# Two transformer blocks on one core: feed-forward rows left undivided by their rms, relu on ScalarE and one square on VectorE, narrower scores of the first row tile

## The chip, the cores and the metric

The kernel runs on one core of a Trainium2 chip. The metric is the device time of one execution in microseconds (us), median over runs. All arithmetic is fp32 in accuracy: an operand is kept as the sum of a high and a low part (`..._hi`, `..._lo`) of the type fp32r, and one product becomes three TensorE matmuls, high by high, high by low and low by high.

## The reference

512 rows of width 1024 go through two blocks. What the change touches is the end of the second block and its windowed attention:

```python
# nsa_mixer: scores of query rows against keys, causal
s_s = jnp.einsum('bqghd,bgqkd->bghqk', qb, k_sel) * scale
s_w = jnp.einsum('bqghd,bkgd->bghqk', qb, kwb) * scale
...
# second_block
x = x + merged @ w_out[l]
h = rms_norm_2(x, norm_mlp[l])          # x * rsqrt(mean(x*x) + eps) * gain
x = x + jnp.square(jax.nn.relu(h @ w_ff1[l])) @ w_ff2[l]
return rms_norm_2(x, norm_final)
```

`w_ff1` is 1024 by 4096 and `w_ff2` 4096 by 1024. With r = rsqrt(mean(x*x) + eps) of a row, relu(r·a)² = r²·relu(a)².

## The kernel before

The hidden width of 4096 is worked off in 8 strips of 512 columns, t = 0 to 7. For a strip, TensorE (PE) multiplies the turned and gained rows by a strip of `w_ff1` in 96 matmuls of 128x512 (`ff_up`, L1111) into four banks of PSUM. VectorE (DVE) makes the activations `h_raw` (shown in the profile as `proj`) from the banks in two passes: `hidden` (L3327) writes max(bank, 0)·r², `square` (L3335) multiplies that by max(bank, 0) again. The factor r² stands in `r_squared`, 128x512, the rows' factors spread over the columns' order of the banks: DVE spreads them into `r_cols`, PE turns these (four transposes of L1034 in the middle of `ff_up(0)`), ScalarE (ACT) copies the bank (L2510) and DVE squares it (L3418).

The second multiplication, rows of `h_raw` by a 512-row strip of `w_ff2`, is done by a Strassen-like scheme of seven products of half-size blocks, twelve matmuls of 128x512 each, in the order 6, 1, 7, 5, 4, 2, 3 (`seven_products`, L1795). The rows' sums and the weights' sums that it needs are made on DVE (`row_sums`, `weight_sums`), their high parts on ACT (`rows_hi`: `a_hi`, `s_hi`; `items_hi`: `item_hi`), their low parts on DVE (`rows_lo`, `weights_lo`, five `item_lo`) and on GpSimd (POOL: the other two `item_lo`, L985). Each finished product lies in two banks, from which DVE adds it into the residual rows or into partial sums (`add_product`, L3355 and L3359). Partial sums are put together at the end (L3436, L3440); the last strip, t = 7, is an ordinary product.

All engines run the same software-pipelined loop, one step per t. PE does `ff_up(t+1)`, then `seven_products(t)`; each engine's order is the order in which its code is written, and semaphores tie them. What a step of DVE, ACT and PE says:

```python
# DVE, ff_step
add_product(i, lambda j: t(j) - 1, 3, 4 * parity)
row_sums(i, t); weight_sums(i, t); rows_lo(i, t); weights_lo(i, t)
hidden(i, lambda j: t(j) + 1)
add_product(i, t, 6, two)
square(i, lambda j: t(j) + 1)
add_product(i, t, 1, one); add_product(i, t, 7, two)
# PE, seven_products: product 5 writes the banks of strip t+1, product 4 those of 6 and 7
elif m == 5:
    pe.wait_ge(sem["emptied_d"], at(i, lambda j: strips_emptied("D", STRIP_FF + 1 + t(j))))
elif m == 4:
    taken(3)
```

`taken(3)` waits until DVE has added three products of this step: 6, 1 and 7. At the end of ACT's step, `his` makes the high parts of four pieces of `w_ff1` for strip t+2 (L1871); each piece comes by a transfer that SP starts when PE has used up the piece before it in the same buffer, four buffers in all. POOL then makes the low parts of the four pieces (L852).

In the attention of the second block, `LARGE_SMALL` units score a row tile i against its keys, as a high-by-high and a high-by-low set of matmuls (L1203, L1205), at least 256 keys wide.

Of the kernel before, what the change touches and what calls it, by code (L numbers as in the profile page):

```python
# [36 lines left out]
P = 128  # L37
# [57 lines left out]
STRIPS = ("A" * 12 + "D" + "AAAA" + "D" + "DD" + "DDDD" * 2 + "DD" + "A" * 6 + "D" * 8 + "DD"  # L95
          + "D" * 8 + "DD")

# [162 lines left out]
def two_block_kernel(  # L260
# [4 lines left out]
    with ExitStack() as ctx:  # L265
# [118 lines left out]
        for name, src, w in (("qb", g_qn_b[0:1, 64:96], 0), ("kb", g_kn_b[0:1, 64:96], 32),  # L384
# [4 lines left out]

        r_squared = place("r_squared", [P, S], where=A)  # L390
        kcv = place("kcv", [32, 2, 2, 64], where=A)
# [16 lines left out]
        stat2 = place("stat2", [P, 32])  # L408
        newton = place("newton", [P, 64])
        kr_sq = place("kr_sq", [P, TT])  # L410
        rstd = place("rstd", [P, 64])
# [33 lines left out]
            "group_done", "group_a", "group_d",  # L445
            "squares", "sq_made", "cq_squares", "b_squares", "mean_made", "root_made", "gate_half", "x_added", "x_turned", "xt_hi", "xt_lo", "r1_spread", "first_half_hi", "gate1_tanh", "r_spread", "r_turned", "r_kept", "gate_tanh", "tile_done", "stat_of", "pow_of", "stat_ready", "pow_done", "dve_step", "sin_in", "sin_out", "half_set",
            "ready_for_t", "qk_ready", "cq_ready", "b_ready", "kc_ready", "q_ready", "ix_scores", "ix_relu", "ix_acc", "z_scaled", "z_ready", "z_tanh",
# [3 lines left out]
            "tanh_in", "tanh_out", "flats", "hid_in", "h_hi", "h_lo", "h_summed", "half_sums",  # L451
            "quarter_in0", "quarter_in1", "quarter_in2", "quarter_in3", "t_made", "item_hi", "item_lo", "item_lo_p", "u_made", "r_squared", "product_done", "product_added", "sums_joined",
            "zeros_set", "keys_twice", "chunk_in0", "chunk_in1", "chunk_summed", "chunk_hi", "chunk_lo", "chunk_out0", "chunk_out1", "row_sums", "sums_hi", "sums_lo", "out_added",
# [551 lines left out]
        def _(pe):  # L1005
# [793 lines left out]
            def seven_products(i, parity, t):  # L1799
# [7 lines left out]
                for m in PRODUCTS:  # L1807
# [28 lines left out]
            def ff_step(i, parity, t):  # L1836

                if not isinstance(i, int):
# [4 lines left out]
                  before=raw_parts(2))  # L1843
            pe.wait_ge(sem["r_kept"], 1)

            ff_step(0, 0, lambda j: 0)
# [16 lines left out]
        def _(act):  # L1863
# [653 lines left out]
            def rows_hi(i, t):  # L2517

                act.wait_ge(sem["emptied_d"], at(i, lambda j: strips_emptied("D", STRIP_FF + t(j))))
                if not isinstance(i, int):  # L2520
# [28 lines left out]
            act.wait_ge(sem["emptied_d"], strips_emptied("D", STRIP_FF + 7))  # L2549
            act.wait_ge(sem["pair_used"], PAIR_LAST)  # L2550
# [28 lines left out]
        def _(dve):  # L2579
# [557 lines left out]
            def add_and_turn(n, s, v):  # L3137
# [16 lines left out]
                dve.wait_ge(sem["pow_done"], powers[0])  # L3154
                dve.tensor_copy(r_cols[:], rstd[:, 0:4].unsqueeze(2).to_broadcast([P, TT, P])).then_inc(sem["r_spread"], 1)

# [163 lines left out]

            def hidden(i, f):

                banks = strip_wait(i, lambda j: STRIP_FF + f(j))
                wait(dve, sem["h_hi"], at(i, lambda j: 3 * f(j)))
                wait(dve, sem["h_lo"], at(i, lambda j: 3 * f(j)))
                for m in range(4):
                    ins = dve.scalar_tensor_tensor(h_raw[:, m, :], banks[m][:], 0.0, r_squared[:], ALU.max, ALU.mult)  # L3327
                ins.then_inc(sem["u_made"], 1)

            def square(i, f):  # L3330

                banks = strip_wait(i, lambda j: STRIP_FF + f(j))
                dve.wait_ge(sem["u_made"], at(i, lambda j: f(j) + 1))
                for m in range(4):
# [12 lines left out]
            def add_product(i, t, m, banks):  # L3347

                dve.wait_ge(sem["product_done"], at(i, lambda j: 7 * t(j) + PRODUCTS.index(m) + 1))
                for u in range(2):  # L3350
# [26 lines left out]
            def row_sums(i, t):  # L3377

                dve.wait_ge(sem["emptied_d"], at(i, lambda j: strips_emptied("D", STRIP_FF + t(j))))
                dve.tensor_tensor(h_sums[:, 2], a11, a21, ALU.subtract)  # L3380
# [11 lines left out]
            def ff_step(i, parity, t):  # L3392
# [40 lines left out]
            dve.wait_ge(sem["product_added"], 49)  # L3433
            upper, lower = proj[:, 0:2, XRES:XRES + D], proj[:, 2:4, XRES:XRES + D]
# [4 lines left out]
            for v, z in ((upper[:, :, S:D], 1), (lower[:, :, S:D], 2)):  # L3439
                ins = dve.tensor_tensor(v, v, part_sums[z][:], ALU.add)  # L3440
            ins.then_inc(sem["sums_joined"], 1)
            dve.wait_ge(sem["sums_joined"], 2)
# [14 lines left out]
            for t in range(TT):  # L3457
                dve.wait_ge(sem["tile_done"], t + 1)
                for k in range(2):
                    v = proj[:, t, XRES + S + 256 * k:XRES + S + 256 * k + 256]  # L3460
                    dve.tensor_tensor(v, v, bank[4 * ((STRIP_LAST + 1) % 2) + t][:, 256 * k:256 * k + 256], ALU.add)\
                       .then_inc(sem["x_added"], 1)
# [39 lines left out]
```

## Time and profile before

| | us |
|---|---|
| median of 3 runs | 1413.48 (1412.42 to 1413.65) |
| the profiled execution | 1412.28 |
| its span in the trace | 1410.5 |
| PE busy | 1400.9 (99% of the span) |
| DVE, ACT, POOL busy | 895.0, 659.6, 634.7 |
| mean granted TensorE clock | 0.998 of full speed |

The span is the time from the first to the last recorded instruction; the execution's own time holds 1.8 us more. Times in the rows are microseconds from the start of the span. Feed-forward runs from about 1072 to 1404.

### The profile page before, as it was taken

To read this page: it belongs to the slowest core of one execution; us is meant where nothing else is said; L and a number is where in the kernel's file an instruction comes from. 1 tells how busy PE (TensorE), PEld (TensorE's weight loads), DVE (VectorE), ACT (ScalarE), POOL (GpSimd) and SP (SyncE) were. 2 spreads that over 40 slices of the span, in tenths; PEclk is the share of its full clock that TensorE was granted. 3 is DMA by queue.
4 is the path that set the end of the run, shared out by engine and by line. 5 is a ranking of instruction groups with operands and counts; after the bars stand their busy time and mean duration, and the time that the engine had idled before them with its cause. 6 is when DMAs were issued, how large, how long until landed. Compare 5 with 4: busy or idle time off the path is not lost.

```text
span 1410.5 us, 20863 instructions
## 1 busy us (share of the span) xinstructions
PE 1400.9 (99%) x7659; PEld 1182.9 (84%) x7659; DVE 895.0 (63%) x1646; ACT 659.6 (47%) x1157; POOL 634.7 (45%) x447
## 2 busy tenths in 40 slices
PE   9999999999999999999999999999999999999998
PEld 8888888778778888899997789988888888888886
DVE  4436998466663384852567678852283977777777
ACT  5544465567573333353343677863235443322342
POOL 4443666645453454154443366754425432344440
PEclk9999999999999999999999999999999999999999
DMA  6332433203102675869672210023275333333221
GB/s 196 99 90 75 148 105 101 66 13 104 37 2 75 209 240 196 292 199 318 237 243 75 76 31 2 2 76 105 90 271 188 114 99 105 104 104 104 91 87 60
DMA packets 90201, 170.28 MB, mean 121 GB/s; under 512 B 8119, under 2 KB 24066, under 8 KB 90114
## 3 DMA queue, kind: packets, MB, share of 16 engines
q1 hardware_dynamic: 80386, 140.72, 31.7%
q10 hardware_dynamic: 9728, 28.39, 5.5%
q8 instruction: 56, 0.92, 0.3%
q14 instruction: 31, 0.25, 0.1%
HBM read 148.12 MB, written 20.97 MB: 120 GB/s over the span
## 4 chain that ended last, share of the span: by engine, by line
PE 99%; DVE 0%; issue 0%; POOL 0%; ACT 0%; POOLq 0%; DVEq 0%; ACTq 0%
PE bank L1111 62%; PE bank L1795 9%; PE bank L1173 5%; PE bank L1387 5%; PE bank L1379 4%; PE bank L1203 4%; PE bank L1034 3%; PE bank L1205 1%; PE bank L1071 1%; PE bank L1612 0%; PE bank L1321 0%; PE bank L1783 0%; PE bank L1339 0%; PE bank L1424 0%; PE bank L1280 0%
## 5 line engine op out<-in xcount | busy, mean ns | idle before, releaser
L852 POOL TENSOR_TENSOR w_lo<-raw,w_hi 128x1024 fp32r<-128x1024 f32 (+3 forms) x185 | 442.7, 2402 | 455.0 <-ACT w_hi L1871 454.7
L1871 ACT ACTIVATE w_hi<-raw 128x1024 fp32r<-128x1024 f32 (+3 forms) x189 | 191.3, 1014 | 361.5 <-DMA raw<-in_w_in 166.0
L1111 PE MATMUL bank<-xt_hi,w_hi 128*128 128x512 f32 x656 | 258.8, 394 | 0.0
L1111 PE MATMUL bank<-xt_hi,w_lo 128*128 128x512 f32 x656 | 255.5, 390 | 0.0
L1111 PE MATMUL bank<-xt_lo,w_hi 128*128 128x512 f32 x656 | 255.4, 389 | 0.0
L1111 PE MATMUL bank<-w_hi,xt_hi 128*128 128x392 f32 (+2 forms) x424 | 153.6, 362 | 0.0
L1111 PE MATMUL bank<-w_lo,xt_hi 128*128 128x392 f32 (+2 forms) x424 | 151.8, 358 | 0.0
L1111 PE MATMUL bank<-w_hi,xt_lo 128*128 128x392 f32 (+2 forms) x424 | 151.8, 358 | 0.0
L1111 PEld LDWEIGHTS bank<-xt_hi,w_hi 128*128 128x128 f32 x656 | 123.2, 188 | 27.0 <-issue 2.4
L1111 PEld LDWEIGHTS bank<-xt_hi,w_lo 128*128 128x128 f32 x656 | 123.1, 188 | 25.8
L1111 PEld LDWEIGHTS bank<-xt_lo,w_hi 128*128 128x128 f32 x656 | 123.3, 188 | 25.2 <-issue 0.5
L985 POOL TENSOR_TENSOR item_lo<-quarter_b,item_hi 128x1024 fp32r<-128x1024 f32 x14 | 33.3, 2400 | 170.8 <-DVE item_lo L3389 170.8
L1111 PEld LDWEIGHTS bank<-w_hi,xt_hi 128*128 128x128 f32 x424 | 79.6, 188 | 7.2 <-issue 0.9
L1111 PEld LDWEIGHTS bank<-w_hi,xt_lo 128*128 128x128 f32 x424 | 79.6, 188 | 6.8
L1111 PEld LDWEIGHTS bank<-w_lo,xt_hi 128*128 128x128 f32 x424 | 79.6, 188 | 6.1
L2137 ACT ACTIVATE sc<-sc,negmax 128x512 f32<-128x512 f32 (+3 forms) x104 | 58.8, 567 | 21.5 <-DVE negmax L2846 21.3
L3355 DVE TENSOR_TENSOR proj<-proj,bank 128x512 f32<-128x512 f32 x56 | 36.0, 683 | 38.7 <-PE bank L1795 38.7
L896 POOL TENSOR_SCALAR proj<-proj,rsum,gsig 128x384 f32<-128x384 f32 (+1 forms) x64 | 38.7, 614 | 40.1 <-DVE rsum L2861 40.1
L2846 DVE CUSTOM_DVE_ANT_0 sc<-bank,cst 128x128 f32<-128x128 f32 (+3 forms) x96 | 43.6, 485 | 15.9 <-PE bank L1203 9.7
L2137 ACT ACTIVATE proj<-proj,negmax 128x384 f32<-128x384 f32 (+1 forms) x80 | 44.0, 552 | 10.5 <-DVE negmax L2846 10.4
L2522 ACT ACTIVATE a_hi<-proj 128x1024 fp32r<-128x1024 f32 x7 | 7.4, 1063 | 85.0 <-PE bank L1795 85.0
L1034 PE MATMUL bank<-cst,proj 128*128 128x128 f32 (+2 forms) x320 | 44.7, 280 | 0.3
(460 smaller groups left out, 3006.7 us busy)
## 6 DMA issues: line engine op xcount, KB each, us to landing
raw<-in_w_in SPq DMA_DIRECT2D x72, 512.0 KB, 3.6
raw<-in_w_ff SPq DMA_DIRECT2D x36, 512.0 KB, 3.7
quarter_b<-in_w_ff SPq DMA_DIRECT2D x28, 512.0 KB, 3.4
raw<-in_w_in SPq DMA_DIRECT2D x24, 392.0 KB, 4.6
w_hi<-sums_hi SPq DMA_DIRECT2D x16, 512.0 KB, 5.0
w_lo<-sums_lo SPq DMA_DIRECT2D x16, 512.0 KB, 5.9
raw<-in_w_branch SPq DMA_DIRECT2D x12, 512.0 KB, 3.7
chunk_a<-in_w_out ACTq DMA_DIRECT2D x12, 512.0 KB, 5.4
```

Of the source, the lines that this page charges most:

```text
L852: pool.tensor_tensor(w_lo[:, slot, 0:halves, 0:width], raw[:, slot, 0:halves, 0:width], w_hi[:, slot, 0:halves, 0:width].bitcast(F32), ALU ...
L896: pool.tensor_scalar(v, v, rsum[:, u % SC:u % SC + 1], gate, ALU.mult, ALU.mult)\
L1034: ins = pe.transpose(b[0:m, o:o + k], src, ident[0:k, 0:k])
L1111: ins = pe.matmul(o, lhs, rhs, start=st and j == 0, stop=en and j == 2)
L1173: ins = pe.matmul(bank[OUT_BANK[m] + u][:], rows[:, 2 * q + kk, u * P:u * P + P], whole[:, slot, kk, :], start=m in (1, 7, 4, 6) and q == ...
L1203: ins = pe.matmul(o, w["q"], w["k"], start=True, stop=w["k_lo"] is None)
L1379: ins = pe.transpose(bank[TURN_BANK + u % 2][0:n, c + t * P:c + (t + 1) * P], src[:, t * P:t * P + n], ident)
L1387: ins = pe.matmul(bank[4 + w["pas"] % 2][w["rows"], w["cols"]], w["v"][t], src[0:n, t * P:(t + 1) * P], start=w["start"] and t == 0, stop= ...
L1795: ins = pe.matmul(bank[banks + u][:], lhs, rhs, start=first and kt == 0 and j == 0, stop=kt == 1 and j == 2, skip_group_check=True)
L1871: act.activation(w_hi[:, slot, 0:halves, 0:width], raw[:, slot, 0:halves, 0:width], ACT.Copy)\
L2137: act.activation(v, v, ACT.Exp, scale=-1.0, bias=negmax[:, u % SC:u % SC + 1], accum_out=sums[:, u % SC:u % SC + 1]).then_inc(sem["exps"], 1)
L2846: dve.tensor_tensor_reduce(sc_of[u % SC][:, 0:w["n"]], bank[b][:, c:c + w["n"]], w["mask"], -w["scale"], BIG, ALU.add, ALU.min, negmax[:, ...
```

## The change

The hidden rows are no longer multiplied by r². ACT writes h = relu(bank) in four instructions 128x512 at the start of its step, before `rows_hi`, then raises the semaphore `relu`; DVE squares `h_raw` in one instruction over 128x4x512 that reads and writes SBUF alone. The factor r² of each row, now 4 columns of the tile `newton`, is put on where the products are added to the residual rows: `add_product` for 2, 3, 4 and 5, the joining of partial sums, and the last strips' additions become a multiply-add with a scalar per row. The spreading of r over rows, its four transposes, its copy and its square (L3418) go. The banks of a feed-forward strip are now given back by ACT, and PE's product 5 waits for that. ACT's loop over t takes two steps an iteration. Scores of the first row tile are 128 keys wide in place of 256, in 32 units of a high and a low matmul each.

```diff
-          + "D" * 8 + "DD")
+          + "A" * 8 + "DD")
...
-            k_hi, k_lo = (part[:, 0:max(i + 1, 2) * P] for part in keys2[g][kind - 1])
+            k_hi, k_lo = (part[:, 0:(i + 1) * P] for part in keys2[g][kind - 1])
...
-                    if r == 2 and kt == 7:
-                        pe.wait_ge(sem["r_spread"], 2)
-                        transposes([(r_cols[:, t, :], P, P) for t in range(TT)])(bank[4]).then_inc(sem["r_turned"], 1)
...
-                        pe.wait_ge(sem["emptied_d"], at(i, lambda j: strips_emptied("D", STRIP_FF + 1 + t(j))))
+                        pe.wait_ge(sem["emptied_a"], at(i, lambda j: strips_emptied("A", STRIP_FF + 1 + t(j))))
...
-            act.wait_ge(sem["r_turned"], 1)
-            act.activation(r_rows[:], bank[4][:], ACT.Copy).then_inc(sem["r_kept"], 1)
...
+            def hidden(i, f):
+
+                banks = strip_wait(i, lambda j: STRIP_FF + f(j))
+                wait(act, sem["h_lo"], at(i, lambda j: 3 * f(j)))
+                wait(act, sem["h_summed"], at(i, f))
+                for m in range(4):
+                    ins = act.activation(h_raw[:, m, :], banks[m][:], ACT.Relu)
+                    if m == 3:
+                        ins.then_inc(sem["emptied_a"], 1)
+                act.wait_ge(sem["emptied_a"], at(i, lambda j: strips_emptied("A", STRIP_FF + f(j))))
+                act.sem_inc(sem["relu"], 1)
...
                 if isinstance(i, int):
                     items_hi(i, t)
+                hidden(i, t)
                 rows_hi(i, t)
...
-            with act.Fori(1, 7) as i:
-                ff_step(i, lambda j: j)
+            with act.Fori(1, 4) as i:
+                ff_step(i, lambda j: 2 * j - 1)
+                ff_step(i, lambda j: 2 * j)
+            hidden(7, lambda j: j)
...
-                    dve.tensor_tensor(v, v, banks[t][:], ALU.add).then_inc(sem["x_added"], 1)
+                    dve.scalar_tensor_tensor(v, banks[t][:], r_squared[:, t:t + 1], v, ALU.mult, ALU.add)\
+                       .then_inc(sem["x_added"], 1)
...
             def square(i, f):
 
-                banks = strip_wait(i, lambda j: STRIP_FF + f(j))
-                dve.wait_ge(sem["u_made"], at(i, lambda j: f(j) + 1))
-                for m in range(4):
-                    ins = dve.scalar_tensor_tensor(h_raw[:, m, :], banks[m][:], 0.0, h_raw[:, m, :], ALU.max, ALU.mult)
-                ins.then_inc(sem["emptied_d"], 1)
+                dve.wait_ge(sem["relu"], at(i, lambda j: f(j) + 1))
+                dve.tensor_tensor(h_raw, h_raw, h_raw, ALU.mult).then_inc(sem["h_made"], 1)
...
                     if o is not None:
-                        ins = dve.tensor_tensor(o, o, bank[banks + u][:], ALU.add)
+                        r = 2 * (m in (4, 5)) + u
+                        ins = dve.scalar_tensor_tensor(o, bank[banks + u][:], r_squared[:, r:r + 1], o, ALU.mult, ALU.add)
...
                 weights_lo(i, t)
-                hidden(i, lambda j: t(j) + 1)
                 add_product(i, t, 6, two)
                 square(i, lambda j: t(j) + 1)
...
-            dve.wait_ge(sem["r_kept"], 1)
-            dve.tensor_tensor(r_squared[:], r_rows[:], r_rows[:], ALU.mult).then_inc(sem["r_squared"], 1)
-            dve.wait_ge(sem["r_squared"], 1)
-            hidden(0, lambda j: 0)
             square(0, lambda j: 0)
...
-            for v, z in ((upper[:, :, S:D], 0), (lower[:, :, 0:S], 0), (lower[:, :, S:D], 0)):
-                ins = dve.tensor_tensor(v, v, part_sums[z][:], ALU.add)
-            ins.then_inc(sem["sums_joined"], 1)
+            def join(z, row, c):
+
+                for u in range(2):
+                    t = 2 * row + u
+                    v = proj[:, t, XRES + S * c:XRES + S * c + S]
+                    ins = dve.scalar_tensor_tensor(v, part_sums[z][:, u, :], r_squared[:, t:t + 1], v, ALU.mult, ALU.add)
+                return ins
```

On ACT, at the seam between two steps of the feed-forward loop, before: the four `w_hi` end step 0 and the next step begins with the rows' high parts (`a_hi`, `s_hi`), then the weights' (`item_hi`).

```order
L2525 ACTIVATE s_hi<-h_sums 128x2048
L1871 ACTIVATE w_hi<-raw 128x1024 x4
L2547 UNCONDITIONAL_BRANCH
L2547 ISA
L2521 REGISTER_ALU
L2522 ACTIVATE a_hi<-proj 128x1024
L2523 ACTIVATE a_hi<-proj 128x512
L2524 REGISTER_ALU
L2525 ACTIVATE s_hi<-h_sums 128x2048
```

And in the changed kernel, at the seam of the two steps inside an iteration (`proj` written from `bank` is `h_raw`):

```order
L1865 ISA
L1866 ACTIVATE w_hi<-raw 128x1024 x2
L1885 REGISTER_ALU
L2526 ACTIVATE proj<-bank 128x512 x4
L2529 REGISTER_ALU
L2512 REGISTER_ALU
L2515 ACTIVATE a_hi<-proj 128x1024
L2516 ACTIVATE a_hi<-proj 128x512
L2518 ACTIVATE s_hi<-h_sums 128x2048
```

The four relus of strip t+1 stand behind the last `w_hi` of step t and ahead of that strip's `a_hi`.

On DVE, in the middle of a step of the loop, from the last `item_lo` to the additions, before (`proj` is `h_raw` in L3327 and L3335, the residual rows in L3355; `part_sum_124`, `_123`, `_125` take products 6, 1, 7):

```order
L3389 TENSOR_TENSOR item_lo_108<-quarter_t_101,item_hi_109 128x1024
L2593 REGISTER_ALU
L3327 SCALAR_TENSOR_TENSOR proj<-bank,r_squared 128x512 x4
L3359 TENSOR_TENSOR part_sum_124<-part_sum_124,bank 128x512 x2
L3333 REGISTER_ALU
L3335 SCALAR_TENSOR_TENSOR proj<-bank,proj 128x512 x4
L3359 TENSOR_TENSOR part_sum_123<-part_sum_123,bank 128x512 x2
L3359 TENSOR_TENSOR part_sum_125<-part_sum_125,bank 128x512 x2
L3355 TENSOR_TENSOR proj<-proj,bank 128x512 x4
```

And in the changed kernel:

```order
L3390 TENSOR_TENSOR item_lo_108<-quarter_t_101,item_hi_109 128x1024
L3360 TENSOR_TENSOR part_sum_124<-part_sum_124,bank 128x512 x2
L3335 REGISTER_ALU
L3336 TENSOR_TENSOR proj<-proj 128x4x512
L3360 TENSOR_TENSOR part_sum_123<-part_sum_123,bank 128x512 x2
L3360 TENSOR_TENSOR part_sum_125<-part_sum_125,bank 128x512 x2
L3356 SCALAR_TENSOR_TENSOR proj<-bank,newton,proj 128x512 x4
```

The eight passes over the banks are gone; one square stands between the addition of product 6 and those of 1 and 7, which stay behind it.

On PE, the scores of the first row tile of a pair of heads in the second block, before:

```order
L1203 MATMUL bank<-k_parts,q_parts 128x512
L1205 MATMUL bank<-k_parts,q_parts 128x512
L1203 MATMUL bank<-k_parts,q_parts 128x256
L1205 MATMUL bank<-k_parts,q_parts 128x256
L1203 MATMUL bank<-k_parts,q_parts 128x256
L1205 MATMUL bank<-k_parts,q_parts 128x256
L1111 MATMUL bank<-beside,w_hi 128x512 x2
```

And in the changed kernel:

```order
L1200 MATMUL bank<-k_parts,q_parts 128x512
L1202 MATMUL bank<-k_parts,q_parts 128x512
L1200 MATMUL bank<-k_parts,q_parts 128x128
L1202 MATMUL bank<-k_parts,q_parts 128x128
L1200 MATMUL bank<-k_parts,q_parts 128x128
L1202 MATMUL bank<-k_parts,q_parts 128x128
L1111 MATMUL bank<-beside,w_hi 128x512 x2
```

The count and the order stay; four matmuls in a row are half as wide.

## Rows read from the trace of the kernel before

**Rows 1.** The page: busy time, share of the span and instructions of each engine.

```profile
PE 1400.9 (99%) x7659; PEld 1182.9 (84%) x7659; DVE 895.0 (63%) x1646; ACT 659.6 (47%) x1157; POOL 634.7 (45%) x447
```

**Rows 2.** The chain that ended last, step t = 2: start, us, what.

```profile
1199.68 19.04 PE bank L1795 x84
```

**Rows 3.** Timeline of DVE in that step: start, us, operation; in brackets idle before, releaser.

```profile
1199.72 2.48 DVE L3327 SCALAR_TENSOR_TENSOR proj<-bank,r_squared 128x512 f32<-128x512 f32 x4 [3.41 <-PE bank L1111]
1202.44 1.28 DVE L3359 TENSOR_TENSOR part_sum<-part_sum,bank 128x512 f32<-128x512 f32 x2 [0.24 <-PE bank L1795]
1203.64 2.48 DVE L3335 SCALAR_TENSOR_TENSOR proj<-bank,proj 128x512 f32<-128x512 f32 x4
...
1207.88 1.28 DVE L3359 TENSOR_TENSOR part_sum<-part_sum,bank 128x512 f32<-128x512 f32 x2 [0.57 <-PE bank L1795]
```

**Rows 4.** Timeline of ACT there: the last `w_hi` of the step.

```profile
1203.41 1.06 ACT L1871 ACTIVATE w_hi<-raw 128x1024 fp32r<-128x1024 f32 x1 [4.24 <-DMA raw<-in_w_ff]
```

**Rows 5.** Timeline of ACT, an eviction of four banks by ACT in the first block.

```profile
150.82 2.07 ACT L1912 ACTIVATE proj<-bank 128x512 f32<-128x512 f32 x4 [0.26 <-PE bank L1111]
```

**Rows 6.** Groups of DVE by line and form: count | busy, mean ns of one.

```profile
L3345 DVE TENSOR_TENSOR s_lo<-h_sums,s_hi 128x2048 fp32r<-128x2048 f32 x7 | 16.0, 2283 | 0.5 <-ACT s_hi L2525 0.5
L3335 DVE SCALAR_TENSOR_TENSOR proj<-bank,proj 128x512 f32<-128x512 f32 x32 | 19.8, 680 | 0.1
```

**Rows 7.** Timeline of POOL in step t = 2.

```profile
1201.19 9.49 POOL L852 TENSOR_TENSOR w_lo<-raw,w_hi 128x1024 fp32r<-128x1024 f32 x4
```

**Rows 8.** Timelines of DVE and POOL elsewhere, operations of SBUF alone on both.

```profile
1097.36 2.89 DVE L3418 TENSOR_TENSOR r_squared<-r_rows 128x512 f32<-128x512 f32 x1
...
1096.72 2.97 POOL L852 TENSOR_TENSOR w_lo<-raw,w_hi 128x1024 fp32r<-128x1024 f32 x1 [4.51 <-ACT w_hi L1871]
...
512.64 2.90 DVE L3165 TENSOR_TENSOR chunk_a<-chunk_a 128x512 f32<-128x512 f32 x1
...
512.34 5.45 POOL L852 TENSOR_TENSOR w_lo<-raw,w_hi 128x1024 fp32r<-128x1024 f32 x2 [3.03 <-ACT w_hi L1871]
```

**Rows 9.** The chain that ended last around strip 0 and the first products.

```profile
1093.12 0.44 PE bank L1034 x4
...
1118.08 19.04 PE bank L1795 x84
```

**Rows 10.** Timelines of ACT and DVE in step t = 0.

```profile
1105.85 2.00 ACT L2536 ACTIVATE item_hi<-quarter_b 128x1024 fp32r<-128x1024 f32 x2
...
1109.21 1.90 ACT L2525 ACTIVATE s_hi<-h_sums 128x2048 fp32r<-128x2048 f32 x1
...
1105.38 0.69 DVE L3380 TENSOR_TENSOR h_sums<-proj 128x512 f32<-128x512 f32 x1
1107.43 0.69 DVE L3383 TENSOR_TENSOR h_sums<-proj,h_sums 128x512 f32<-128x512 f32 x1
1113.36 1.22 DVE L3389 TENSOR_TENSOR item_lo<-quarter_t,item_hi 128x1024 fp32r<-128x1024 f32 x1
```

**Rows 11.** Timeline of PE, scores of a first row tile.

```profile
827.52 0.28 PE L1203 MATMUL bank<-k_parts,q_parts 128*128 128x256 f32 x1
...
828.00 0.60 PE L1379 MATMUL bank<-cst,proj 128*128 128x128 f32 x4
```

**Rows 12.** Timeline of PE's weight loads (PEld): full weights for 16-column matmuls.

```profile
737.20 0.75 PEld L1673 LDWEIGHTS bank<-proj 128*128 128x128 f32 x6
```

**Rows 13.** Timeline of PE: 128-wide plain fp32 matmuls, four in the program, eight records.

```profile
413.30 1.05 PE L1387 MATMUL bank<-prob_t,kvm 128*128 128x128 f32 x8
```

**Rows 14.** Timeline of DVE at the end: the joining of sums and the next addition.

```profile
1384.63 3.50 DVE L3436 TENSOR_TENSOR proj<-proj,part_sum 128x1024 f32<-128x1024 f32 x3
...
1393.08 2.48 DVE L3090 TENSOR_TENSOR proj<-proj,bank 128x512 f32<-128x512 f32 x4 [2.56 <-PE bank L1111]
```

**Rows 15.** Windows after the last matmul: busy PE, PEld, DVE, ACT, POOL; PEclk (granted clock).

```profile
1404.00:1406.00 2.00, 0.00 (x0) 0.00 (x0) 1.93 (x6) 1.52 (x5) 0.13 (x1) 1.00 0.68 262
1406.00:1410.50 4.50, 0.00 (x0) 0.00 (x0) 0.57 (x2) 0.72 (x1) 0.54 (x1) 0.51 0.62 233
```

More of the change, by code:

```diff
@@ L388, in two_block_kernel @@
         allow = place("allow", [P, 1280 - P])
-        r_squared = place("r_squared", [P, S], where=A)
         kcv = place("kcv", [32, 2, 2, 64], where=A)
@@ L409, in two_block_kernel @@
         newton = place("newton", [P, 64])
+        r_squared = newton[:, 0:TT]
         kr_sq = place("kr_sq", [P, TT])
@@ L445, in two_block_kernel @@
             "group_done", "group_a", "group_d",
-            "squares", "sq_made", "cq_squares", "b_squares", "mean_made", "root_made", "gate_half", "x_added", "x_turned", "xt_hi", "xt_lo", "r1_spread", "first_half_hi", "gate1_tanh", "r_spread", "r_turned", "r_kept", "gate_tanh", "tile_done", "stat_of", "pow_of", "stat_ready", "pow_done", "dve_step", "sin_in", "sin_out", "half_set",
+            "squares", "sq_made", "cq_squares", "b_squares", "mean_made", "root_made", "gate_half", "x_added", "x_turned", "xt_hi", "xt_lo", "r1_spread", "first_half_hi", "gate1_tanh", "r_spread", "gate_tanh", "tile_done", "stat_of", "pow_of", "stat_ready", "pow_done", "dve_step", "sin_in", "sin_out", "half_set",
             "ready_for_t", "qk_ready", "cq_ready", "b_ready", "kc_ready", "q_ready", "ix_scores", "ix_relu", "ix_acc", "z_scaled", "z_ready", "z_tanh",
@@ L451, in two_block_kernel @@
             "tanh_in", "tanh_out", "flats", "hid_in", "h_hi", "h_lo", "h_summed", "half_sums",
-            "quarter_in0", "quarter_in1", "quarter_in2", "quarter_in3", "t_made", "item_hi", "item_lo", "item_lo_p", "u_made", "r_squared", "product_done", "product_added", "sums_joined",
+            "quarter_in0", "quarter_in1", "quarter_in2", "quarter_in3", "t_made", "item_hi", "item_lo", "item_lo_p", "relu", "h_made", "product_done", "product_added", "sums_joined",
             "zeros_set", "keys_twice", "chunk_in0", "chunk_in1", "chunk_summed", "chunk_hi", "chunk_lo", "chunk_out0", "chunk_out1", "row_sums", "sums_hi", "sums_lo", "out_added",
@@ L1843, in _ @@
                   before=raw_parts(2))
-            pe.wait_ge(sem["r_kept"], 1)
             ff_step(0, 0, lambda j: 0)
@@ L2517, in rows_hi @@
             def rows_hi(i, t):
-                act.wait_ge(sem["emptied_d"], at(i, lambda j: strips_emptied("D", STRIP_FF + t(j))))
+                act.wait_ge(sem["h_made"], at(i, lambda j: t(j) + 1))
                 if not isinstance(i, int):
@@ L2546, in _ @@
             ff_step(0, lambda j: 0)
-            with act.Fori(1, 7) as i:
-                ff_step(i, lambda j: j)
-            act.wait_ge(sem["emptied_d"], strips_emptied("D", STRIP_FF + 7))
+            with act.Fori(1, 4) as i:
+                ff_step(i, lambda j: 2 * j - 1)
+                ff_step(i, lambda j: 2 * j)
+            hidden(7, lambda j: j)
+            act.wait_ge(sem["h_made"], 8)
             act.wait_ge(sem["pair_used"], PAIR_LAST)
@@ L3154, in add_and_turn @@
                 dve.wait_ge(sem["pow_done"], powers[0])
-                dve.tensor_copy(r_cols[:], rstd[:, 0:4].unsqueeze(2).to_broadcast([P, TT, P])).then_inc(sem["r_spread"], 1)
+                if n == 0:
+                    dve.tensor_copy(r_cols[:], rstd[:, 0:4].unsqueeze(2).to_broadcast([P, TT, P])).then_inc(sem["r_spread"], 1)
+                else:
+                    step(dve.tensor_tensor(r_squared, rstd[:, 0:4], rstd[:, 0:4], ALU.mult))
             def sum_chunk(c):
@@ L3319, in _ @@
             a11, a12, a21, a22 = h_raw[:, 0:2, 0:256], h_raw[:, 2:4, 0:256], h_raw[:, 0:2, 256:512], h_raw[:, 2:4, 256:512]
-            def hidden(i, f):
-                banks = strip_wait(i, lambda j: STRIP_FF + f(j))
-                wait(dve, sem["h_hi"], at(i, lambda j: 3 * f(j)))
-                wait(dve, sem["h_lo"], at(i, lambda j: 3 * f(j)))
-                for m in range(4):
-                    ins = dve.scalar_tensor_tensor(h_raw[:, m, :], banks[m][:], 0.0, r_squared[:], ALU.max, ALU.mult)
-                ins.then_inc(sem["u_made"], 1)
-            def square(i, f):
-                banks = strip_wait(i, lambda j: STRIP_FF + f(j))
-                dve.wait_ge(sem["u_made"], at(i, lambda j: f(j) + 1))
-                for m in range(4):
-                    ins = dve.scalar_tensor_tensor(h_raw[:, m, :], banks[m][:], 0.0, h_raw[:, m, :], ALU.max, ALU.mult)
-                ins.then_inc(sem["emptied_d"], 1)
+            def square(i, f):
+                dve.wait_ge(sem["relu"], at(i, lambda j: f(j) + 1))
+                dve.tensor_tensor(h_raw, h_raw, h_raw, ALU.mult).then_inc(sem["h_made"], 1)
             def rows_lo(i, t):
@@ L3377, in row_sums @@
             def row_sums(i, t):
-                dve.wait_ge(sem["emptied_d"], at(i, lambda j: strips_emptied("D", STRIP_FF + t(j))))
+                dve.wait_ge(sem["h_made"], at(i, lambda j: t(j) + 1))
                 dve.tensor_tensor(h_sums[:, 2], a11, a21, ALU.subtract)
@@ L3433, in _ @@
             dve.wait_ge(sem["product_added"], 49)
-            upper, lower = proj[:, 0:2, XRES:XRES + D], proj[:, 2:4, XRES:XRES + D]
-            for v, z in ((upper[:, :, S:D], 0), (lower[:, :, 0:S], 0), (lower[:, :, S:D], 0)):
-                ins = dve.tensor_tensor(v, v, part_sums[z][:], ALU.add)
-            ins.then_inc(sem["sums_joined"], 1)
+            def join(z, row, c):
[4 more added lines that the diff above has]
+                return ins
+            join(0, 0, 1)
+            join(0, 1, 0)
+            join(0, 1, 1).then_inc(sem["sums_joined"], 1)
             dve.wait_ge(sem["sums_joined"], 1)
-            for v, z in ((upper[:, :, S:D], 1), (lower[:, :, S:D], 2)):
-                ins = dve.tensor_tensor(v, v, part_sums[z][:], ALU.add)
-            ins.then_inc(sem["sums_joined"], 1)
+            join(1, 0, 1)
+            join(2, 1, 1).then_inc(sem["sums_joined"], 1)
             dve.wait_ge(sem["sums_joined"], 2)
@@ L3460, in _ @@
                     v = proj[:, t, XRES + S + 256 * k:XRES + S + 256 * k + 256]
-                    dve.tensor_tensor(v, v, bank[4 * ((STRIP_LAST + 1) % 2) + t][:, 256 * k:256 * k + 256], ALU.add)\
+                    dve.scalar_tensor_tensor(v, bank[4 * ((STRIP_LAST + 1) % 2) + t][:, 256 * k:256 * k + 256],
+                                             r_squared[:, t:t + 1], v, ALU.mult, ALU.add)\
                        .then_inc(sem["x_added"], 1)
```

## The prediction

> **What bounds the kernel now.** I read the page first: TensorE is busy for 1400.9 of 1410.5 us [rows 1]. The chain that ended last says the same, and in the feed-forward loop it holds nothing but TensorE: a step's seven products (84 matmuls, 19.04 us, 0.2267 each) follow the matmuls of the strip without a piece of another engine between [rows 2]. So nothing that the change saves on VectorE, ScalarE or GpSimd shortens the kernel by itself. It can only win by matmuls removed or narrowed, and lose wherever TensorE has to wait. Of such waits the loop has two that the change touches. Product 5 waits until the banks of strip t+1 are empty, product 4 until three additions (6, 1, 7) are done. Counted from the start of the products, 1199.68, product 5 comes after 36 matmuls, at 1207.84, and product 4 after 48, at 1210.56 [rows 2]. The timeline of VectorE shows the third addition ending at 1207.88 + 1.28 = 1209.16, because it can't begin before product 7 is done [rows 3]. So 1.4 us are spare at product 4. That is all the room that the middle of the step has.
>
> **The middle of a step.** Before, VectorE worked through 2.48 + 1.28 + 2.48 us of passes and additions there, all from banks that TensorE had filled already [rows 3]. Now the square waits for the relus, and these stand in ScalarE's queue behind the last `w_hi` of the step. That one waits for its transfer, and runs from 1203.41 to 1204.47 [rows 4], long after strip t+1 was finished at 1199.68. The ring of four buffers behind it isn't changed, so it stays there. Four relus from banks: the nearest row is ScalarE's eviction of four banks of the same shape, 2.07 us [rows 5]. They run from 1204.4 to 1206.45; with about 0.1 us for the wait on their own end, the square may begin at 1206.6. Product 5, due at 1207.84, gets its banks 1.3 us in time.
>
> The square is one instruction with 2048 columns, both inputs and the output in SBUF. The nearest row, a subtraction of that shape, takes 2.28 us [rows 6]. Alone it would end at 1208.9. The additions of 1 and 7 stand behind it in VectorE's order, each some 1.2 us: the third ends at 1211.4. Product 4 would be 0.9 to 1.0 us late.
>
> But it isn't alone. GpSimd is making the low parts of four weight pieces from 1201.19 to 1210.68, 2.37 us each, so its third runs from 1205.93 to 1208.30 [rows 7]. What two such operations do to each other stands elsewhere in the trace. A 128x512 multiplication of VectorE, in SBUF alone, was begun at 1097.36 and took 2.89 us [rows 8], where one of that shape takes 0.69 [rows 10]; it ended half a microsecond after GpSimd's operation (1096.72 to 1099.69), as if it had only then begun. At 512.64 the same: 2.90 us beside two operations of GpSimd, which for their part took 2.73 each in place of 2.4 [rows 8]. The passes of before read a bank, and they ran beside those same low parts at 680 ns, with no such delay [rows 6, 7]. So I take it that the square, ready at 1206.6, begins when GpSimd's third operation ends, at 1208.3, and GpSimd's fourth begins when the square ends. Square until 1210.6, additions until 1213.0, product 4 at 1213.1 in place of 1210.5: TensorE stands for **2.6 us**. GpSimd's fourth low part ends at 1213 in place of 1210.7, and is wanted only in a later step, hidden. The Trainium skill, page "SBUF — State Buffer", section "Who interferes with whom", states the same as a rule: the port pair that VectorE's second SBUF input and GpSimd share is locked for a whole instruction. By it the stall is that of the locked square; without it, that of the free one. This trace agrees, with its 2.89 us.
>
> Steps 1 to 6 have this: 6 x 2.6 = **+15.6 us**. Every stall shifts all engines alike (transfers start from TensorE's progress), so none is paid for by the one before.
>
> **Step 0.** Four transposes go, 0.44 us [rows 9]. But `h_raw` of strip 0 is now made behind ScalarE's seven `item_hi`, which end at 1107.85 [rows 10], about 1107.4 once everything is 0.44 earlier. Relus until 1109.5 [rows 5], square until 1111.9 [rows 6]. Then the old row of steps: row sums 2.74 (1105.38 to 1108.12 before), `s_hi` 1.90 [rows 10], `s_lo` 2.28 [rows 6], the first `item_lo` 1.22: 1120.1 with a little for semaphores. TensorE is there at 1118.08 - 0.44 = 1117.64 [rows 9]. Before, that `item_lo` ended at 1114.6 [rows 10], so the 3.4 us of room are used up, and 2.5 more. The middle of step 0 has the same square with the rest of the step late; I take 0.6 us for it, between 0 and the 2.6 of other steps. Sum of step 0: 2.5 + 0.6 - 0.44 = **+2.7**.
>
> **Scores.** 32 units with a high and a low matmul, 64 in all, go from 256 to 128 columns. Four of 256 take 0.48 us, 0.12 each [rows 11]. How fast the narrow ones go isn't in the trace for this type. From below: if the time fell by width alone, from 0.227 at 512 and 0.12 at 256, it would be about 0.06, and 64 would save 3.8 us. From above: a plain fp32 product of 128 columns shows as two records, and eight of them, 1.05 us with the last one's length of 0.275, come every 0.11: 0.22 a product [rows 13]; if the narrow ones were run that way, they would cost 64 x 0.10 = 6.4 us more. Between them I take what a full set of weights costs when the moving side is tiny: six loads for matmuls of 16 columns in 0.75 us, with one's own length of 0.19, one every 0.11 [rows 12]. The narrow matmuls stand four in a row, each with weights of its own, so 64 x 0.007 = **-0.4 us**. The Trainium skill, page "TensorE: Matmul & The Clock Gate", section "LDWEIGHTS (loading the stationary operand)", has 107 ns for a load of 128 columns, which agrees with the 0.11. Its section "Back-to-back issue gap" has 81 ns a matmul at 128 columns in a sustained stream; by that the 64 would save 2.5 us in place of 0.4.
>
> **What lies beside other work, at nothing.** The factor in `add_product` makes a two-operand addition a three-operand one of the same shape with a bank: such a form took 2.48 us for four where the addition takes 1.28 for two [rows 3]. They are product 5, 4, 2, 3, after each of which VectorE waits for TensorE; without that cover it would be some 0.05 us each. The joins become ten of 0.6 where five took 1.17: 6.0 for 5.85 us, before 2.56 us of idle [rows 14]. The copy on ScalarE and L3418 go from engines that don't bound. The two-step loop on ScalarE changes nothing that it issues.
>
> **The clock.** After the last matmul (before 1404) the granted clock stayed at full up to 1406 and was half after that [rows 15]. Within the kernel no wait before was long enough to see it fall. Six waits of 2.6 us are at the edge of what that end shows. A fall puts matmuls at 1.2 GHz for a while, each taking twice as long, and how long is in no row: from nothing to another stall's length each, 0 to 15.6 in all. I take **+3**, a fifth of that.
>
> **Sum.** 1412.28 + 15.6 + 2.7 - 0.4 + 3 = 1433.2. The profiled execution lies 1.2 us under the median of 1413.48, so the median comes to 1434.
>
> **Rivals.**
> - A, forecast: the square waits behind GpSimd's third low part. For it, [rows 3 to 8]. Without the clock 1431.4, with all of its price 1447. Chance 0.62.
> - B: the square isn't held, because it gets in between two of GpSimd's operations or because the two don't exclude each other in this form. Stalls of 1.0 us: 6.0 + 2.7 - 0.4 = +8.3, 1421.8. For it, that the relus end within 0.7 us of GpSimd's second boundary, 1205.93; against it, that they would have to be 0.7 us earlier. Chance 0.15.
> - C: the narrow scores run like plain fp32, +6.4 on A in place of -0.4: 1438 to 1441. For it only that the code held them at 256. Chance 0.12.
> - D: no stall, because the relus are done early enough, say for a last transfer that lands 2.5 us sooner. The third addition then ends by 1210.5, and all that is left is under 3 us at step 0, or nothing: within 0.2%. Against it, [rows 4]. Chance 0.06.
> - E, the other side: the narrow scores gain by width, 3.8 us, and the loop doesn't stall. 1413.5 - 3.8 - 0.44 = 1409.3, if step 0 is hidden too. It decides if all stalls together stay under 1.4 us, which asks the third addition to end by 1210.5 in every step. Chance 0.05.
>
> **The numbers.** 0.2% of this kernel, 2.8 us, is about what a measurement can tell. A, B and C are slower, 0.89; D is same, 0.06; E is faster, 0.05. The range takes in B at its low end, 1421, and C and most of the clock's price at the upper end, 1443; D, E and a full fall of the clock are left out.
>
> **What would show it.** In the changed kernel's timeline each step has ScalarE's last `w_hi`, four relus about 2.07 us, a square of some 4.0 us in the records (begun at 1206.6 relative to a product start at 1199.68, its wait counted in), two additions, and a gap of 2.6 us on TensorE before product 4 that VectorE's L3360 released. If the square shows 2.3 us and the gap 1 us, it is B. If the matmuls of L1200 and L1202 of 128 columns come every 0.11 us, the scores are right; at 0.06 it is E's gain, at 0.2 C. At the first products a gap of 2.5 us, released by VectorE. I am wrong if ScalarE's last `w_hi` moves forward or back with the change, if relu costs other than a copy, or if the clock falls in most steps.

## The result and the profile after

The changed kernel takes 1436.78 us (median of 6 runs, 1435.66 to 1437.53), the kernel before 1412.89 (6 runs). The ratio is 1.017, with a 95% interval of 1.0159 to 1.0181: 24 us slower.

The page of the changed kernel, engines by busy time:

```profile
span 1434.8 us, 20823 instructions
PE 1405.2 (98%) x7655; PEld 1182.0 (82%) x7655; DVE 874.6 (61%) x1594; ACT 675.0 (47%) x1188; POOL 643.7 (45%) x447
```

VectorE works 20 us less than in [rows 1] and ScalarE 15 us more. Neither says anything of the 24 us. The chain that ended last does: where [rows 2] had nothing but TensorE, a step (t = 2) now reads

```profile
1206.74 3.75 DMA raw<-in_w_ff
1211.48 2.05 ACT proj L2526 x4
1213.60 3.87 DVE proj L3336
1217.47 2.40 DVE part_sum L3360 x4
1220.01 8.41 PE bank L1792 x36
```

The last weight piece lands, ScalarE makes its high part, then the relus; VectorE squares, adds products 1 and 7, and only then TensorE goes on, with product 4. ScalarE there, to be set beside [rows 4]:

```profile
1210.52 1.06 ACT L1866 ACTIVATE w_hi<-raw 128x1024 fp32r<-128x1024 f32 x1 [4.42 <-DMA raw<-in_w_ff]
1211.48 2.04 ACT L2526 ACTIVATE proj<-bank 128x512 f32<-128x512 f32 x4
```

The timelines of VectorE and GpSimd answer to [rows 3] and [rows 7]:

```profile
1209.33 1.28 DVE L3360 TENSOR_TENSOR part_sum<-part_sum,bank 128x512 f32<-128x512 f32 x2 [6.01 <-PE bank L1792]
1213.60 3.87 DVE L3336 TENSOR_TENSOR proj<-proj 128x2048 f32<-128x2048 f32 x1 [2.99 <-ACTq L2530]
1217.39 2.47 DVE L3360 TENSOR_TENSOR part_sum<-part_sum,bank 128x512 f32<-128x512 f32 x4
...
1208.19 11.50 POOL L852 TENSOR_TENSOR w_lo<-raw,w_hi 128x1024 fp32r<-128x1024 f32 x4
```

GpSimd's four operations take 11.50 us in place of 9.49. At 2.37 each the third ends at 1215.3, and 2.2 us after that, at 1217.47, the square ends, close to the 2.28 that it takes alone. The two don't share the time. The third operation of GpSimd, beside which the square's record begins, has 2.4 us in its own record, as when alone, and the fourth, beside the square, has 4.4. On TensorE's timeline the two matmuls on either side of the gap:

```profile
1217.07 0.39 PE L1792 MATMUL bank<-item_hi,s_lo 128*128 128x512 f32 x1
1220.01 0.47 PE L1792 MATMUL bank<-item_hi,a_hi 128*128 128x512 f32 x1 [2.56 <-DVE part_sum L3360]
```

Between their starts lie 2.94 us in place of the pitch of 0.23: 2.7 us lost. The same gap, 2.92 to 2.94, stands in each of steps 1 to 6, and one of 2.76 (from 1117.51 to 1120.27) before the first products. The clock fell after three of the seven. Windows behind the gap of step 5 (busy PE, PEld, DVE, ACT, POOL; PEclk):

```profile
1352.00:1353.00 1.00, 0.60 (x2) 0.53 (x3) 1.00 (x3) 0.00 (x0) 0.07 (x1) 0.74 0.00 0
1353.00:1355.00 2.00, 2.00 (x6) 1.53 (x5) 0.57 (x1) 0.00 (x0) 0.00 (x0) 0.50 0.00 0
1355.00:1356.00 1.00, 1.00 (x4) 0.79 (x3) 0.00 (x0) 0.00 (x0) 0.00 (x0) 0.55 0.00 0
1356.00:1358.00 2.00, 2.00 (x11) 1.60 (x10) 0.97 (x2) 0.00 (x0) 0.00 (x0) 1.00 0.00 0
```

Half clock, 1.2 GHz, for a little over 3 us. In the chain such a piece is longer for the same count of matmuls: 10.05 us for 36 (10.01 in step 3), where the four steps without a fall have 8.4, and 20.93 for the 84 of step 0. Before, these 84 took 19.2 us, counted in the same way from the start of the first of them (1117.92 on TensorE's timeline): 1.7 less.

```profile
1120.27 20.93 PE bank L1792 x84
...
1352.40 10.05 PE bank L1792 x36
```

### The profile page after: what moved, and what is told of

Same layout as the page of the kernel before. It is cut to its first block, busy times and chain, and to the rows that moved or that the text cites. A ratio compares the mean times of both kernels' runs of the same rounds, so it can differ in the third digit from the quotient of the medians.

```text
span 1434.8 us, 20823 instructions
## 1 busy us (share of the span) xinstructions
PE 1405.2 (98%) x7655; PEld 1182.0 (82%) x7655; DVE 874.6 (61%) x1594; ACT 675.0 (47%) x1188; POOL 643.7 (45%) x447
## 4 chain that ended last, share of the span: by engine, by line
PE 90%; DVE 4%; DMA 3%; ACT 2%; issue 1%; POOL 0%; SPq 0%; ACTq 0%; POOLq 0%; DVEq 0%
PE bank L1111 59%; PE bank L1173 5%; PE bank L1792 5%; PE bank L1384 4%; PE bank L1376 4%; PE bank L1200 4%; PE bank L1034 3%; DVE proj L3336 2%; DMA raw<-in_w_ff 2%; PE bank L1202 1%; PE bank L1071 1%; DVE part_sum L3360 1%; ACT proj L2526 1%; DMA raw<-in_w_in 1%; PE bank L1609 0%
## 5 line engine op out<-in xcount | busy, mean ns | idle before, releaser
L852 POOL TENSOR_TENSOR w_lo<-raw,w_hi 128x1024 fp32r<-128x1024 f32 (+3 forms) x185 | 449.3, 2437 | 459.8 <-ACT w_hi L1866 459.6
L2132 ACT ACTIVATE sc<-sc,negmax 128x512 f32<-128x512 f32 (+3 forms) x104 | 58.8, 566 | 20.9 <-DVE negmax L2854 20.5
L3356 DVE SCALAR_TENSOR_TENSOR proj<-bank,newton,proj 128x512 f32<-128x512 f32 x56 | 39.4, 744 | 34.1 <-PE bank L1792 34.1
L1792 PE MATMUL bank<-item_hi,a_hi 128*128 128x512 f32 x84 | 34.5, 411 | 15.2 <-DVE part_sum L3360 15.2
```

Of the source, the lines that this page charges most:

```text
L852: pool.tensor_tensor(w_lo[:, slot, 0:halves, 0:width], raw[:, slot, 0:halves, 0:width], w_hi[:, slot, 0:halves, 0:width].bitcast(F32), ALU ...
L1792: ins = pe.matmul(bank[banks + u][:], lhs, rhs, start=first and kt == 0 and j == 0, stop=kt == 1 and j == 2, skip_group_check=True)
L2132: act.activation(v, v, ACT.Exp, scale=-1.0, bias=negmax[:, u % SC:u % SC + 1], accum_out=sums[:, u % SC:u % SC + 1]).then_inc(sem["exps"], 1)
L3356: ins = dve.scalar_tensor_tensor(o, bank[banks + u][:], r_squared[:, r:r + 1], o, ALU.mult, ALU.add)
```

## The experiments

Seven kernels, each measured beside the kernel before on the same chip. Ratios are to that kernel.

### pool_yields: GpSimd keeps off until the square is done

```diff
                 for q in range(4):
+                    if q == 2 and made is not None:
+                        pool.wait_ge(sem["h_made"], at(i, made))
                     split(at(i, lambda j: p0(j) + q), (PAIR_FF + q) % RING, 2, S, PAIR_FF)
...
-                ff1_lo(i, lambda j: PAIR_FF + 8 + 4 * j)
+                ff1_lo(i, lambda j: PAIR_FF + 8 + 4 * j, lambda j: j + 2)
```

> The changed kernel, but in the loop GpSimd makes the third and fourth weight low of a step only after the square. Theory (the square is held by GpSimd's third operation): the square takes 2.3 us in place of 3.9, each of the six gaps of 2.9 us between matmul starts falls to 1.3, which is 1.6 x 6 = 9.6 us, and no gap of the loop is long enough for the clock to fall, 3.2 us more: about 1424 us. Rival (the square is slow in its own right, one operand read twice): it still takes 3.9 us and the time stays at 1437.

Measured: 1422.89 us, ratio 1.0075 (1.0058 to 1.0092). Timelines of VectorE and GpSimd in step 2:

```profile
1209.74 2.29 DVE L3338 TENSOR_TENSOR proj<-proj 128x2048 f32<-128x2048 f32 x1 [2.81 <-ACTq L2532]
1211.95 2.47 DVE L3362 TENSOR_TENSOR part_sum<-part_sum,bank 128x512 f32<-128x512 f32 x4
...
1206.85 2.41 POOL L852 TENSOR_TENSOR w_lo<-raw,w_hi 128x1024 fp32r<-128x1024 f32 x1
1212.20 4.74 POOL L852 TENSOR_TENSOR w_lo<-raw,w_hi 128x1024 fp32r<-128x1024 f32 x2 [2.93 <-DVE proj L3338]
```

With GpSimd idle the same square takes 2.29 us. The gaps of the loop are 1.18 to 1.33 us, one 0.86. The rival, a square that is slow by itself, is out: it was GpSimd's operation that held it for 1.6 us. What stays, about 1 us a step, is the relus' lateness and the order on VectorE. In the profiled execution, 1420.98 us, the clock never fell before the last matmul. The other three took 1422.87 to 1423.91; a fall would make such a difference, but no trace of them shows whether there was one.

### square_after_one: one addition less behind the square

```diff
                 add_product(i, t, 6, two)
-                square(i, lambda j: t(j) + 1)
                 add_product(i, t, 1, one)
+                square(i, lambda j: t(j) + 1)
                 add_product(i, t, 7, two)
```

> The changed kernel with the addition of product 1 ahead of the square. Theory (the two additions behind the square are part of each stall): the square ends where it did, one addition of 1.2 us less stands behind it, the gaps fall from 2.9 to 1.7 us: 7.2 us, and the two falls of the clock in the loop go, 3.2 us: about 1426. Rival (product 4 waits for something else than the third addition): 1437.

Measured: 1426.61 us, ratio 1.0097 (1.008 to 1.0114). VectorE, then the matmuls beside the gap:

```profile
1214.70 3.99 DVE L3336 TENSOR_TENSOR proj<-proj 128x2048 f32<-128x2048 f32 x1
1218.61 1.27 DVE L3360 TENSOR_TENSOR part_sum<-part_sum,bank 128x512 f32<-128x512 f32 x2
...
1218.30 0.39 PE L1792 MATMUL bank<-item_hi,s_lo 128*128 128x512 f32 x1
1220.03 0.47 PE L1792 MATMUL bank<-item_hi,a_hi 128*128 128x512 f32 x1 [1.34 <-DVE part_sum L3360]
```

The square is held as long as ever, the gap is 1.73 us in place of 2.94: the one addition that no longer stands behind it. The profiled execution, 1428.75, is the slowest of the four; it holds one more wait, 1.71 us between two starts at 1074.66, ahead of the feed-forward strips and of the edit.

### square_last: square behind all three additions

```diff
                 add_product(i, t, 6, two)
-                square(i, lambda j: t(j) + 1)
                 add_product(i, t, 1, one)
                 add_product(i, t, 7, two)
+                square(i, lambda j: t(j) + 1)
```

> The changed kernel with the square behind the additions of 6, 1 and 7. Theory: none of the six gaps is left, 16.2 us and the two falls of the clock 3.2 us: about 1417, with the gap of 2.8 us at the first products and its fall of the clock still there. Rival (a late square gives a new wait: the addition of product 5 or the row sums of the next step come late): a gap at product 3 or at the next products, 1 us or more a step, 1423 or more.

Measured: 1415.79 us, ratio 1.0023 (1.0014 to 1.0033). VectorE in step 2:

```profile
1211.36 1.28 DVE L3360 TENSOR_TENSOR part_sum<-part_sum,bank 128x512 f32<-128x512 f32 x2 [1.43 <-PE bank L1792]
1212.56 3.86 DVE L3336 TENSOR_TENSOR proj<-proj 128x2048 f32<-128x2048 f32 x1
1216.34 2.71 DVE L3356 SCALAR_TENSOR_TENSOR proj<-bank,newton,proj 128x512 f32<-128x512 f32 x4
1219.52 1.41 DVE L3356 SCALAR_TENSOR_TENSOR proj<-bank,newton,proj 128x512 f32<-128x512 f32 x2 [0.46 <-PE bank L1792]
```

The square is still held to 3.86 us, and TensorE doesn't notice: no gap of the loop is left. The additions behind it come late, but VectorE is idle again from 1219.05 to 1219.52, and no new wait appears. Only the gap before the first products is there, 2.75 us, and the low clock behind it.

### square_last_relu0: the relus of strip 0 ahead of the item highs

```diff
                 if isinstance(i, int):
+                    hidden(i, t)
                     items_hi(i, t)
-                hidden(i, t)
+                else:
+                    hidden(i, t)
                 rows_hi(i, t)
```

Beside this it has the order of square_last on VectorE.

> The kernel of square_last, with the relus of strip 0 on ScalarE ahead of the seven item highs of step 0. Theory (the gap before the first products is the relus' place behind the item highs): no gap of over 1 us is left from 1000 us on, 2.5 us of stall and about 2 us of low clock less than square_last: 1411.3, by 0.5 to 1.5 under the kernel before. Rival (step 0 is held by the chain from square over row sums and their parts, wherever the relus stand, or the item highs now come late): a gap of 1 us or more remains, 1413 or more.

Measured: 1411.81 us, ratio 0.9991 (0.9982 to 1.0). ScalarE in step 0, and TensorE at the seam of strip 1 and the first products:

```profile
1101.04 2.04 ACT L2526 ACTIVATE proj<-bank 128x512 f32<-128x512 f32 x4
1111.33 1.91 ACT L2518 ACTIVATE s_hi<-h_sums 128x2048 fp32r<-128x2048 f32 x1
...
1117.70 0.39 PE L1111 MATMUL bank<-xt_hi,w_lo 128*128 128x512 f32 x1
1117.92 0.39 PE L1792 MATMUL bank<-item_hi,s_hi 128*128 128x512 f32 x1
```

The relus run at 1101.0 in place of 1107.6, the first product follows its strip at the pitch, and no gap is left. The items are 2 us later than before and `s_hi` with them, within the room of step 0.

### relu_early: VectorE as changed, relus ahead of the last weight high

```diff
                 if isinstance(i, int):
+                    hidden(0, lambda j: 0)
                     items_hi(i, t)
-                hidden(i, t)
                 rows_hi(i, t)
...
-                his(i, lambda j: PAIR_FF + 8 + 4 * t(j))
+                his(i, lambda j: PAIR_FF + 8 + 4 * t(j), 3)
+                hidden(i, lambda j: t(j) + 1)
+                his(i, lambda j: PAIR_FF + 8 + 4 * t(j), 4, q0=3)
...
-            hidden(7, lambda j: j)
```

Here `his` got a first piece, `q0`, and the relus of strip 0 stand ahead of the item highs. So this run holds two moves; that the one in step 0 has its own effect, square_last and square_last_relu0 show.

> The changed kernel with VectorE's order as it was changed (square ahead of the additions of 1 and 7), but with the four relus between the third and the last weight high on ScalarE, and those of strip 0 ahead of the item highs. Theory (the relus' lateness behind the last weight high starts the stall): the square is ready 2.9 us sooner, is held by GpSimd's second operation in place of its third, and the third addition ends some 11 us after the start of the products, where product 4 is due: gaps of at most 0.5 us more than the pitch, no fall of the clock, 1411 to 1414. Rival (the held square alone makes the stall, wherever it begins): gaps of 1.5 us or more in each step, 1421 or more.

Measured: 1412.23 us, ratio 0.9996 (0.9987 to 1.0005). ScalarE, VectorE and GpSimd in step 2:

```profile
1199.53 2.07 ACT L2526 ACTIVATE proj<-bank 128x512 f32<-128x512 f32 x4 [0.80 <-PE bank L1111]
...
1203.32 2.28 DVE L3337 TENSOR_TENSOR proj<-proj 128x2048 f32<-128x2048 f32 x1
1207.55 1.28 DVE L3361 TENSOR_TENSOR part_sum<-part_sum,bank 128x512 f32<-128x512 f32 x2 [0.76 <-PE bank L1792]
...
1200.98 11.59 POOL L852 TENSOR_TENSOR w_lo<-raw,w_hi 128x1024 fp32r<-128x1024 f32 x4
```

The time came as expected, by a way that I had wrong. The square wasn't held by GpSimd's second operation: it came at 1203.32, just before that one began (1200.98 + 2.37 = 1203.35), took 2.28 us, and GpSimd did the waiting (11.59 for four in place of 9.49); so it went in all six steps, each time by 0.02 to 0.03 us. What it stood behind was no longer the relus, done at 1201.60, but the addition of product 6. The third addition waits for its product again, as in [rows 3], and TensorE has no gap in the loop or before it.

### factor_only: the factor at the outputs, both passes on VectorE

```diff
+                for m in range(4):
+                    ins = dve.tensor_scalar(h_raw[:, m, :], banks[m][:], 0.0, None, ALU.max)
+                ins.then_inc(sem["h_made"], 1)
...
-                dve.tensor_tensor(h_raw, h_raw, h_raw, ALU.mult).then_inc(sem["h_made"], 1)
...
+                for m in range(4):
+                    ins = dve.scalar_tensor_tensor(h_raw[:, m, :], banks[m][:], 0.0, h_raw[:, m, :], ALU.max, ALU.mult)
+                ins.then_inc(sem["emptied_d"], 1)
```

> The changed kernel with relu and square on VectorE from the banks in two passes, as before, but with the factor at the outputs and the narrow scores. Theory (the factor at the outputs is hidden beside other work): no gap anywhere, 1412 us, 0.5 to 1.5 under the kernel before. Rival (multiply-adds at the outputs cost 0.13 us a pair more and delay the end or a product): some 2 us or more over the kernel before.

Measured: 1411.85 us, ratio 0.9996 (0.9986 to 1.0006). TensorE has no gap in the feed-forward. A multiply-add with a scalar per row is dearer than an addition, at the end too. The last joins of the kernel before, which belong to [rows 14], then this kernel:

```profile
1388.16 2.36 DVE L3440 TENSOR_TENSOR proj<-proj,part_sum 128x1024 f32<-128x1024 f32 x2
```

```profile
1384.20 6.84 DVE L3436 SCALAR_TENSOR_TENSOR proj<-part_sum,newton,proj 128x512 f32<-128x512 f32 x10
1392.52 2.73 DVE L3084 SCALAR_TENSOR_TENSOR proj<-bank,newton,proj 128x512 f32<-128x512 f32 x4 [1.49 <-PE bank L1111]
```

Ten joins take 6.84 us where the five of before took 3.50 + 2.36; one microsecond of the idle time in [rows 14] is gone, 1.49 is left. So the factor, the transposes and the narrow scores together change nothing that can be measured.

### scores_alone: the narrow scores in the kernel before

```diff
-            k_hi, k_lo = (part[:, 0:max(i + 1, 2) * P] for part in keys2[g][kind - 1])
+            k_hi, k_lo = (part[:, 0:(i + 1) * P] for part in keys2[g][kind - 1])
```

> The kernel before with the narrower scores of the first row tile alone. My theory (weights set the pace): 0.11 us a matmul, 0.4 to 1.3 us less in all, inside what the measurement can tell. Rival by width: 3.8 us less, 1409. Rival (they are run in several passes): 6 us more, 1419.

Measured: 1411.86 us, ratio 0.9993 (0.9984 to 1.0002). TensorE at one group of four:

```profile
886.38 0.22 PE L1203 MATMUL bank<-projr 128*128 128x128 f32 x1
886.43 0.28 PE L1205 MATMUL bank<-projr 128*128 128x128 f32 x1
886.54 0.28 PE L1203 MATMUL bank<-projr 128*128 128x128 f32 x1
886.66 0.28 PE L1205 MATMUL bank<-projr 128*128 128x128 f32 x1
```

The second starts 0.05 us after the first, then one every 0.11 to 0.12. Both rivals, 1409 and 1419, are out, and so is the saving of 2.5 us that the prediction names beside its own sum.

The time can't tell so small a gain from zero, but the traces can. The same two matmuls of 512 columns, one ahead of these scores and one behind them, start at 819.98 and 937.96 before and at 819.41 and 937.04 here: 117.98 and 117.63 us apart. In the changed kernel it is 117.64, in square_last_relu0 117.63. The scores save 0.35 us, where 0.4 was forecast.

## Why the prediction was right, step by step

It was right in its mechanism, its sign and nearly its size: 1434 forecast, 1436.8 measured. The account in the trace, by spans (1410.5 to 1434.8, 24.3 us):

| term | forecast | seen |
|---|---|---|
| six stalls before product 4 | 6 x 2.6 = 15.6 | 6 x 2.8 = 16.8 |
| step 0: before the first products | 2.5 | 2.76 - 0.23 = 2.5 |
| step 0: its middle | 0.6 | none |
| step 0: transposes gone | -0.44 | -0.5 |
| low clock | 3 | 1.7 + 1.6 + 1.6 = 4.9 |
| scores | -0.4 | -0.35 |
| waits ahead of the feed-forward | none | 0.6 |
| sum | 20.9 | 24.0 |

The stalls are counted from strip to strip. In the chain, before and then changed:

```profile
1199.68 19.04 PE bank L1795 x84
1218.72 21.76 PE bank L1111 x96
...
1184.82 21.77 PE bank L1111 x96
...
1228.41 21.77 PE bank L1111 x96
```

A step takes 43.59 us in place of 40.80, 2.8 more; 2.7 of it is the gap between two starts, and 0.1 more goes with it. The transposes are read from two matmuls of `ff_up(0)` on either side of them, 1090.00 and 1100.02 before, 1090.31 and 1099.83 changed. The 0.6 us ahead of the feed-forward belong to no term of the change: the largest part is one wait of 0.5 us near 814, ahead of the scores, and it differs from run to run, from nothing in relu_early to 1.1 us in square_after_one. The 0.3 us that is left over stands in no term.

**The held square** was shown: with GpSimd quiet it takes 2.29 us, beside it 3.87. What the section "Who interferes with whom" of the page "SBUF — State Buffer" in the Trainium skill states, a lock for a whole instruction, is what both traces show, from both sides: in the changed kernel the square waits for GpSimd's operation, in relu_early GpSimd's waits for the square (11.59 us for four in place of 9.49).

**It needed all three.** The stall is 2.7 us because the relus stand behind the last weight high, because the square is held, and because two additions stand behind the square. Moving the relus alone removes it, moving the square alone removes it, taking the hold away leaves about 1.1 us a step. That last is rival B's world, which pool_yields made: B's sum was 8.3 us, and the profiled execution of pool_yields, in which the clock didn't fall, has a span 8.7 us longer than before (1419.2 and 1410.5).

**The middle of step 0** had no loss, where 0.6 us was forecast, and that is luck. After the first gap TensorE ran at half clock, its products took 1.7 us longer, and the third addition, done at 1131.69, came before product 4, which started at 1132.87. One loss covered another. Where the clock didn't fall, in pool_yields, the loss is there: product 4 starts 0.52 us after the matmul before it, in place of 0.23.

```profile
1130.21 0.39 PE L1794 MATMUL bank<-item_hi,s_lo 128*128 128x512 f32 x1
1130.73 0.47 PE L1794 MATMUL bank<-item_hi,a_hi 128*128 128x512 f32 x1
```

**The clock** was the term that I had least for: bounds of 0 and 15.6, and 3 taken, a guess. Three falls of 1.6 to 1.7 us came, 4.9 in all. The price of one was bounded at a stall's length, 2.6, and is 1.6 to 1.7; how many there would be, nothing on record told. The falls follow only the gaps of over 2.6 us: after the first-products gap of 2.76 in the changed kernel, and of 2.75 and 2.61 in square_last and square_after_one; but not after a gap of 2.76 in pool_yields, nor after four of the six of 2.93 here. None followed the gaps of 1.2 to 1.8 us. What decides between two gaps of one length stays open. In square_last the low clock began 0.8 us after the first matmul behind the gap (1119.67): of this window 0.5 us were at half clock.

```profile
1119.00:1121.00 2.00, 1.33 (x5) 1.13 (x6) 2.00 (x3) 0.00 (x0) 0.00 (x0) 0.87 0.63 219
```

**"At nothing"** held for the time, not for the price: I had the multiply-add with a scalar per row at the addition's 0.64 us, from a form without such a scalar. It takes 1.41 us for two, where the addition takes 1.28, and the ten joins take 6.84 us in factor_only where I had 6.0. The idle time of VectorE behind each covers it.

**No version is clearly better than the kernel before.** square_last_relu0, with 0.9991 and an interval that reaches 1.0, is the best of the changed form. VectorE is busy for 881.8 us in it, 13 less than before, and TensorE, busy for 99% in either, has no use for that.

## What to carry to other kernels

Where the critical engine is full, work taken from another one gains nothing, and a move pays for its place in two queues: ask what it stands behind on the new engine, and what stands behind it on the old one. A VectorE operation with two inputs from SBUF, put where GpSimd works from SBUF, must be priced with GpSimd's operation in front of it; the passes of before, which read a bank and one tile, ran beside it without delay. When a wait is needed, put ahead of it what others wait for: one line moved behind two others gave back 21 of 24 us.

## What the runs showed of the hardware

- A low clock of half speed came after five of ten gaps of 2.6 to 2.9 us between two matmul starts. It began 0.1 us after the first matmul behind the gap in the changed kernel, 0.6 in square_after_one and 0.8 in square_last, and lasted a little over 3 us; 1.6 to 1.7 us were lost each time in the changed kernel. Gaps of 1.2 to 1.8 us never brought one.
- A hold between VectorE and GpSimd goes by who comes first: where the square began 0.02 us ahead of GpSimd's next operation it took 2.28 us and the other waited, 4.5 us in its record in place of 2.4 (relu_early); where it came during one, it waited for that one's end, 3.87 us in the record (changed kernel). The wait shows as a longer instruction, not as idle time.
- Four narrow fp32r matmuls with weights of their own: the second follows after 0.05 us, the others at 0.11 to 0.12, the pitch of the weight loads in [rows 12].
